# One comparison of 2048 columns for both one-hots of a gate group, and the scaling split three to five

## The reference, cut to what matters

```
top_s, top_i = lax.top_k(scores, PEER_TOPK)                 # two halves, 128 keys each
cand_s = top_s[..., 0, :, None] + top_s[..., 1, None, :]
best_s, best_pos = lax.top_k(cand_s, PEER_TOPK)
best_i = jnp.take_along_axis(cand_i, best_pos, axis=-1)     # = i1 * 128 + i2
gate = jax.nn.softmax(best_s, axis=-1)
...
u = jnp.take(expert_u, ib, axis=0)
act = jax.nn.gelu(jnp.einsum('td,tkd->tk', xb, u), approximate=False)
return jnp.einsum('tk,tkd->td', (gb * act), vv)
```

## Time and profile before

| | us |
|---|---|
| median of 3 runs (lowest, highest) | 3183.58 (3179.44, 3187.36) |
| the profiled execution, its own time | 3182.52 |
| its span, first to last instruction | 3180.7 |
| PE, DVE, ACT, POOL busy | 3011.1, 2027.4, 1264.7, 1202.9 |
| the gate stage, from its first comparison to its last DMA of gates | 762.4 to 923.5 |

### The profile page before, as it was taken

One profiled execution on the slowest core, in us unless ns is written; L12 is line 12 of the kernel. 1 busy time (PEld: TensorE's weight loads), 2 busy tenths in 40 slices (PEclk: granted clock), 3 DMA queues, 4 the chain that ended last, 5 costly groups with the idle time before them and its releaser, 6 DMA issues.

```text
span 3180.7 us, 47766 instructions
## 1 busy us (share of the span) xinstructions
PE 3011.1 (95%) x17737; PEld 2623.4 (82%) x17737; DVE 2027.4 (64%) x3225; ACT 1264.7 (40%) x2171; POOL 1202.9 (38%) x576
## 2 busy tenths in 40 slices
PE   5998899998989999999999999899999999999998
PEld 2766578998888888888887788699999975899976
DVE  4576614999978778788886355466651465466622
ACT  2347433445963333333333334432222446432221
POOL 1520233675225444455553312044434530244443
PEclk8998999999999999999999999699999999999999
DMA  5630123555579999999996211032223220122321
GB/s 215 231 132 1 48 92 89 169 170 179 221 251 345 345 334 343 334 350 349 344 341 227 66 47 47 7 93 91 87 86 97 84 80 1 41 93 92 92 92 68
DMA packets 181093, 507.07 MB, mean 159 GB/s; under 512 B 15840, under 2 KB 73184, under 8 KB 176736
## 3 DMA queue, kind: packets, MB, share of 16 engines
q1 hardware_dynamic: 72000, 262.18, 25.1%
q0 software_dynamic: 36864, 134.23, 11.3%
q10 hardware_dynamic: 72096, 108.93, 10.2%
HBM read 465.43 MB, written 39.85 MB: 159 GB/s over the span
## 4 chain that ended last, share of the span: by engine, by line
PE 84%; DVE 6%; ACT 6%; issue 2%; DMA 1%; ACTq 0%; DVEq 0%
PE ps L1274 23%; PE ps L1225 17%; PE ps L1162 15%; PE ps L1522 8%; PE ps L897 6%; ACT arena L1938 2%; PE ps L1339 2%; PE ps L947 1%; PE ps L1405 1%; ACT arena L1954 1%; PE ps L1669 1%; DVE arena L2344 1%; PE ps L1412 1%; PE ps L1292 1%; PE ps L1448 1%
## 5 line engine op out<-in xcount | busy, mean ns | idle before, releaser
L2292 POOL TENSOR_TENSOR w_lo<-ring,w_hi 128x1024 fp32r<-128x1024 f32 x312 | 789.5, 2533 | 1547.0 <-ACT w_hi L793 1546.6
L793 ACT ACTIVATE w_hi<-ring 128x1024 fp32r<-128x1024 f32 x500 | 525.4, 1055 | 780.5 <-PE ps L1225 264.0
L1225 PE MATMUL ps<-w_hi,arena_r 128*128 128x512 f32 x1536 | 427.3, 397 | 5.2 <-DVE arena_r L2730 5.2
L1162 PE MATMUL ps<-h_hi,w_hi 128*128 128x384 f32 x1024 | 354.9, 347 | 4.6 <-issue 4.6
L1274 PE MATMUL ps<-h_hi,w_hi 128*128 128x264 f32 (+2 forms) x1536 | 348.2, 299 | 4.8 <-DVE arena L2827 4.8
L1225 PEld LDWEIGHTS ps<-w_hi,arena_r 128*128 128x128 f32 x1536 | 289.2, 189 | 73.3 <-DVE arena_r L2730 6.0
L1162 PE MATMUL ps<-h_lo,w_hi 128*128 128x384 f32 x1024 | 348.3, 340 | 0.0
L1274 PE MATMUL ps<-h_lo,w_hi 128*128 128x264 f32 (+2 forms) x1536 | 347.1, 298 | 0.0
L1274 PE MATMUL ps<-h_hi,w_lo 128*128 128x264 f32 (+2 forms) x1536 | 346.4, 298 | 0.0
L1162 PE MATMUL ps<-h_hi,w_lo 128*128 128x384 f32 x1024 | 345.8, 338 | 0.0
L2719 DVE TENSOR_TENSOR w_lo<-ring,w_hi 128x1024 fp32r<-128x1024 f32 x188 | 228.5, 1222 | 134.1 <-ACT w_hi L793 132.7
(11 more groups left out here) (343 smaller groups left out, 5487.7 us busy)
## 6 DMA issues: line engine op xcount, KB each, us to landing
ring<-weight_stream SPq DMA_DIRECT2D x500, 512.0 KB
gates<-arena ACTq DMA_DIRECT2D x12, 2048.0 KB, 7.2
arena<-gates ACTq DMA_DIRECT2D x32, 768.0 KB, 14.4
arena<-w_modulation ACTq DMA_DIRECT2D x16, 1024.0 KB, 5.2
early_acts<-arena ACTq DMA_DIRECT2D x64, 192.0 KB
arena<-early_acts ACTq DMA_DIRECT2D x32, 384.0 KB, 7.4
arena<-w_modulation ACTq DMA_DIRECT2D x4, 2048.0 KB, 24.3
x<-x_t ACTq DMA_DIRECT2D x1, 2048.0 KB, 11.8
```

The lines of the kernel that those rows point to most:

```text
L793: act.activation(w_hi[:, s, :], ring[:, s, :], ACT.Copy).then_inc(hi_ready, 1)
L1162: last = pe.matmul(ps[:, bank, 0:ND], w, v, start=c == 0 and p == 0, stop=c == DC - 1 and p == 2)
L1225: last = pe.matmul(ps[:, Y_BANKS[b][half], :], a[u], w[v][:, half * BANK:(half + 1) * BANK], start=first and p == 0, stop=final and p == 2)
L2292: pool.tensor_tensor(w_lo[:, s, :], ring[:, s, :], w_hi[:, s, :], ALU.subtract)\
```

## The change

Both one-hots of a group are made by one comparison of 2048 columns (2 x 8 x 128) into a new buffer `hot12`, of which there are two. For that the index tables lie side by side (`idx12`). The wait for PE, which stood ahead of the second comparison, now stands ahead of the joint one, beside the wait for ACT; `hot1_made` is given when the joint comparison has ended. `SCALED` goes from 6 to 5: ACT scales five tokens of a group, DVE the other three (384 columns). Everything else stays.

```
-SCALED = 6
+SCALED = 5
...
-        idx2 = view(2112, ND)
-        gate_t = view(2496, ND)
-        idx1 = view(2880, ND)
+        idx12 = view(2112, 2, ND)
+        idx1, idx2 = idx12[:, 0, :], idx12[:, 1, :]
+        gate_t = view(2880, ND)
...
-        hot2 = view(12640, 2, GROUP, NKEYS)
-        hot1g = view(14688, 2, GROUP, NKEYS)
-        hot1 = [view(16736 + 1024 * k, GROUP, NKEYS) for k in range(2)]
+        hot12 = [view(12640 + 2048 * k, 2, GROUP, NKEYS) for k in range(2)]
+        hot1g = view(16736, 2, GROUP, NKEYS)
...
-                    last = pe.matmul(ps[:, k % 4, t * P:(t + 1) * P], hot2[:, k // 2 % 2, at_t, :],
+                    last = pe.matmul(ps[:, k % 4, t * P:(t + 1) * P], hot12[k // 2 % 2][:, 1, at_t, :],
                                      hot1g[:, k // 2 % 2, at_t, :], start=True, stop=True)
...
-                    last = act.activation(hot1g[:, g % 2, t, :], hot1[g % 2][:, t, :], ACT.Identity,
+                    last = act.activation(hot1g[:, g % 2, t, :], hot12[g % 2][:, 0, t, :], ACT.Identity,
                                           scale=gate_t[:, k:k + 1])
...
                 t = slice(GROUP * g, GROUP * (g + 1))
-                wide = [P, GROUP, NKEYS]
-                iota = cst("iota").unsqueeze(1).broadcast_to(wide)
+                wide = [P, 2, GROUP, NKEYS]
                 wait(dve, hot_scaled, g - 1)
-                dve.tensor_tensor(hot1[g % 2], idx1[:, t].unsqueeze(2).broadcast_to(wide), iota, ALU.is_equal)\
-                    .then_inc(hot1_made, 1)
                 wait(dve, g_made, 2 * (g - 1))
-                dve.tensor_tensor(hot2[:, g % 2], idx2[:, t].unsqueeze(2).broadcast_to(wide), iota, ALU.is_equal)
+                dve.tensor_tensor(hot12[g % 2], idx12[:, :, t].unsqueeze(3).broadcast_to(wide),
+                                  cst("iota").unsqueeze(1).unsqueeze(1).broadcast_to(wide), ALU.is_equal).then_inc(hot1_made, 1)
                 dve.wait_ge(hot1_made, g + 1)
                 rest = slice(GROUP * g + SCALED, GROUP * (g + 1))
-                dve.tensor_tensor(hot1g[:, g % 2, SCALED:, :], hot1[g % 2][:, SCALED:, :],
+                dve.tensor_tensor(hot1g[:, g % 2, SCALED:, :], hot12[g % 2][:, 0, SCALED:, :],
                                   gate_t[:, rest].unsqueeze(2).broadcast_to([P, GROUP - SCALED, NKEYS]), ALU.mult)\
                     .then_inc(hot_ready, 1)
```

## The result

The changed kernel takes **3210.7 us** (median of 4 runs, 3204.6 to 3213.7) against 3184.03 (median of 4, 3179.44 to 3187.36): slower by a ratio of 1.0084, 95% interval 1.0067 to 1.0101. The profiled execution took 3211.3 us, its span is 3209.3.

A forecast was written before the change was run, and what follows sets the result against it. ACT was taken to set the gate stage's 12.79 us step, DVE nearly full; a 14.75 period gives +3, +19.6 and +0.7, +23.3 on 3182.5, about 3206. Forecast range 3199 to 3213 (0.60); wider range 3190 to 3216.

The forecast's parts named there:

- (1): ACT in the gate stage: one scaling fewer per group saves 0.293 us, its step falling from 12.78 to 11.61.
- (2): DVE's joint comparison: 2.29 us, next start after 2.33, against 2.28 for two comparisons, so the merge saves nothing.
- (3): DVE's scaling of three tokens: 0.465 us instead of 0.33, making DVE's step 13.38, 0.59 above 12.79.
- (4): Moved wait for PE closes a DVE-ACT-PE loop over two groups: 6.74 us a turn, 13.5 per step.
- (5): POOL's 2.2 us hold of DVE falls into the closed loop, giving a gate-stage period of 14.75 us.
- The chain that I wrote down ahead: Gate-stage step followed from ACT's first group through POOL's hold and one loop turn: links summing to 14.82 us.
- my expected signs: Expected in the changed profile: POOL spacing 14.6 to 14.9, some comparisons about 4.4, PE waiting for ACT, clock 1.00.
- D: Rival: gaps drop PE to its 1.2 GHz clock throughout the stage, +122 us, 3305; chance 0.04.
- (6): Ends of the gate stage: first step about +3, ten steps +19.6, last step +0.7, in all +23.3 us.
- A: Rival: DVE's throughput alone sets the gate stage's period at 13.38, +7 us, 3191; chance 0.11.
- B: Rival: POOL's hold falls outside the loop, period 13.5 to 14.0, +9 to +15 us, about 3196; chance 0.14.
- C: Rival: hold hidden in DVE's waits and loop short, so ACT's relief gains 14 us, 3169; chance 0.06.

The follow-up runs named there:

- E1: Kernel before with SCALED 5 alone (two comparisons and their waits stay, DVE scales three tokens): 3184.1 us, ratio 1.0000, period 13.14 us.
- E4: Changed kernel with three joint-comparison buffers instead of two and five gathered-row buffers instead of six: 3186.9 us, ratio 1.0018 to the kernel before.
- E6: Kernel before with only the wait for PE moved ahead of the first comparison: 3194.5 us, ratio 1.0036.
- E2: Changed kernel with SCALED back at 6, so the joint comparison alone: 3216.6 us, ratio 1.0108 to the kernel before.
- E3: Changed kernel with POOL's subtraction in the stage cut from 1024 to 16 columns: 3198.6 us in one run, period 14.04 us.
- E9: Kernel before with the stage's low parts on DVE instead of POOL, SCALED still 6: 3181.6 us, ratio 1.0003.
- E5: Kernel before with SCALED 5 and the stage's low parts on DVE instead of POOL: 3174.7 us, ratio 0.9974.

## Why the prediction was right

The forecast was 3206 and slower; the measured 3210.7 lies 5 above, and the ratio's interval is +21 to +32 us, against the +23.3 worked out. One slip in its arithmetic: 3205.8 and 1.1 are 3206.9, so its own sum says 3207. Point by point:

(1) Scaling: five take 1.58 (1.57 forecast); ACT's relief bought nothing by itself, as E1 shows.

(2), (3) The joint comparison took 2.29 and the scaling behind it started 2.32 later (2.33); the scaling of three tokens takes 0.56 and, by the starts in E4 (855.57 + 0.47), costs 0.47 (0.465). By the Trainium skill's rule on one large tile ("VectorE: DVE Perf Modes", section on the TRN2 errata) the merge should have paid 0.13 per group, an estimate from the durations. The trace bears the rule out for durations (2.29 against 2 x 1.21), not for what a group costs DVE: E4's group takes 2.80 by its starts, E1's, with two comparisons, 2.74.

(4) The closed loop is the main cause. It is shown from three sides: the moved wait alone costs 0.94 per step (E6), a third buffer takes back 1.62, of the loop and of the hold in it together (E4), and more work for ACT makes the changed kernel slower while the same work makes the kernel before no slower (E2, E1).

(5) POOL's hold falls into the loop: 0.82 of the 2.06 (E3). The chain that I wrote down ahead came out link by link: 3.47 (3.46), 2.33 (2.3), 2.32 (2.32), 1.81 (1.80), 2.70 (2.62), 2.32 (2.32). The one link that was sized too small is the way from PE's two batches to DVE, 0.08. The second link, 0.1 and a hold of 2.2 in the prediction, is right in its sum and wrong in its parts: the comparison is ready only 1.03 behind POOL's start, since it waits for PE, and POOL adds 1.30. Any readiness within POOL's turn gives the same 2.33, so the forecast of the period did not suffer by it. Three of my expected signs were off. The held comparison is not 4.4 long but 3.5 to 3.6, for that reason; in the second and third step it is not even the comparison that is held but the scaling, 2.59 and 2.60 for 0.56. PE's idle time is put down to ACT in 25 places, not in nearly every group; in the settled steps PE waits ahead of three groups of four. And the clock was not 1.00 from the second step on (see D below).

(6) The ends. Until the first gelu +3.2 (+3 forecast), ten steps +21.5 (+19.6), the last step +0.9 (+0.7), together 25.6 against 23.3. The ten steps are where most of the 2.3 was missed: 1.96 per step should have been 2.06, and the first two of them ran at 15.3 before the loop settled. Of the 28.6 between the two spans, 4.4 had come about before the stage began (its first comparison starts at 766.84, not 762.41), where nothing is changed; it starts between 759.7 and 766.9 in all eleven profiled executions, changed or not, so that is scatter. Behind the stage the changed kernel was 1.4 quicker. In the medians the difference is 26.7.

The rivals: A's 13.38 is about what E4 reached by a third buffer (13.24), not what the changed kernel did. B and C had the hold outside the loop; E3 and E4 show it in it. D did not happen as a state that lasts: the clock stayed at 1.00 over nine steps in which PE waited ahead of most groups. But it fell a second time, which it did not do in the kernel before. Behind the first DMA of gates PE stood still for 2.70 us, and the next batch ran at the lower level (1.2 GHz), 2.04 instead of 1.05 (granted clock 0.63 in 792 to 796). Timeline of PE, changed kernel, then of DVE, the held scaling of point (5):

```profile
793.41 2.04 PE L1203 MATMUL ps<-arena 128*128 128x128 f32 x8 [2.70 <-issue]
```

```profile
792.62 2.59 DVE L2677 TENSOR_TENSOR arena<-arena 128x384 f32<-128x384 f32 x1
```

No loss of time can be read from it: the step in which it fell took 15.26 (791.29 to 806.55), the next 15.33. The Trainium skill's "TensorE: Matmul & The Clock Gate", section on HAM oscillation, has idle gaps between short bursts bring the low clock. The gap of 2.70 agrees; gaps of 0.6 to 1.7 us in the nine steps did not bring it, and neither did one of 2.66 at the same place in E3.

## What to carry to other kernels

When an instruction is merged with its neighbour, write down what each of the two waited for and who waited for each: the merged one inherits both waits and gives its result at the end of both. If that closes a circle over the buffers, the sum of one turn divided by the number of buffers is the new bound, and it can exceed every engine's own work, as 14.86 does here, where the fullest engine, DVE with POOL's hold, has 13.24 to do (E4). The turn alone gives 13.5; ACT's end of step and the hold bring the rest. And where two engines are both full, relieving one measures as nothing; find the second edit before discarding the first (E1, E9, and both in E5).

## What the runs showed of the hardware that I had not expected

POOL doesn't always get its turn behind the DVE instruction that is running. In E1 (timelines of POOL and DVE) its subtraction is recorded from 833.32 for 6.97 us, though it needs 2.36 undisturbed; five DVE instructions passed it, and it got through when DVE stood still for 0.57. Six of the twelve steps of E1 have such a record:

```profile
833.32 6.97 POOL L2292 TENSOR_TENSOR w_lo<-ring,w_hi 128x1024 fp32r<-128x1024 f32 x1 [6.17 <-ACT w_hi L793]
```

```profile
833.63 0.55 DVE L2680 TENSOR_TENSOR arena<-arena 128x384 f32<-128x384 f32 x1
834.10 1.22 DVE L2674 TENSOR_TENSOR arena<-arena,const 128x1024 f32<-128x1024 f32 x1
835.23 1.22 DVE L2677 TENSOR_TENSOR arena<-arena,const 128x1024 f32<-128x1024 f32 x1
836.37 0.55 DVE L2680 TENSOR_TENSOR arena<-arena 128x384 f32<-128x384 f32 x1
836.83 1.22 DVE L2674 TENSOR_TENSOR arena<-arena,const 128x1024 f32<-128x1024 f32 x1
838.63 2.74 DVE L2677 TENSOR_TENSOR arena<-arena,const 128x1024 f32<-128x1024 f32 x1 [0.57 <-PE ps L1204]
```

In the next step of the same kernel POOL started at 846.45 and held the very next DVE instruction (L2680 at 846.76, 2.71). What decides between the two I can't say: no run was made for it.

The Trainium skill, "SBUF — State Buffer", section "Who interferes with whom", has the port that DVE and GpSimd share as an exclusive lock held for a whole instruction. The held instructions shown here agree with that; the five that passed POOL are not covered by it. The cost is lopsided too: POOL's 1024 columns keep a DVE that has work from it for 2.06 (E4) to 2.2 us, and DVE does the same 1024 columns in 1.14.
